# Two mixers in one program: the norm factors, the row factors and the first transposes at the passage from the first to the second

## The reference

```python
# end of the first block: mix is (512 x 2048)
out = jnp.einsum('bse,ed->bsd', mix, w_out[layer])
x = layer_norm(alpha * x + out, ln_g[layer], ln_b[layer])   # (u-mu)*rsqrt(var+eps)*g + b

# begin of the second block
mod = cond @ ada_w[i] + ada_b[i]
shift, scale, gate = jnp.split(mod, 3, axis=-1)
hdn = rms_norm_2(x, norm_g[i]) * (1.0 + scale[:, None, :]) + shift[:, None, :]
proj = h @ w_in                                             # h = hdn, w_in is 1024 x 6176
```

## Time and profile before

| what | us |
|---|---|
| median of 3 runs (lowest, highest) | 1112.73 (1109.14, 1112.83) |
| the profiled execution, device time | 1113.06 |
| its span in the profile | 1111.3 |
| TensorE matmul busy | 1067.0 (96%) |
| VectorE busy | 660.3 (59%) |
| ScalarE busy | 442.5 (40%) |
| GpSimd busy | 210.5 (19%) |

### The profile page before, as it was taken

How to read it: one execution, slowest core, us unless ns; L and a number is a source line. 1 busy time by engine, 2 the same in 40 slices (tenths; PEclk the granted TensorE clock), 3 DMA queues, 4 the chain that set the end, 5 groups by cost and what they waited for, 6 DMA issues and landing times. The chain is left out here.

```text
span 1111.3 us, 14437 instructions
## 1 busy us (share of the span) xinstructions
PE 1067.0 (96%) x5558; PEld 877.2 (79%) x5558; DVE 660.3 (59%) x1137; ACT 442.5 (40%) x824; POOL 210.5 (19%) x159
## 2 busy tenths in 40 slices
PE   7999999999989999989899999999999998999997
PEld 4888888888778867778778788887878876888886
DVE  4246435641156598655737865766594667876635
ACT  4223224332256553231523343348622447425432
POOL 0000000000000142201400100002104664135792
PEclk9999999999989999989999999999999999999999
DMA  8276534322132041132324345435211222203501
GB/s 298 82 265 226 202 114 133 114 76 94 30 123 58 19 177 39 38 128 81 118 81 151 114 150 190 153 114 171 84 68 45 89 95 76 76 20 98 188 1 77
DMA packets 58306, 123.89 MB, mean 111 GB/s; under 512 B 5760, under 2 KB 6016, under 8 KB 58112
## 3 DMA queue, kind: packets, MB, share of 16 engines
q1 hardware_dynamic: 55792, 110.22, 29.4%
q0 software_dynamic: 2304, 12.58, 3.2%
q10 hardware_dynamic: 144, 0.20, 0.0%
HBM read 108.83 MB, written 14.16 MB: 111 GB/s over the span
## 5 line engine op out<-in xcount | busy, mean ns | idle before, releaser
L287 DVE TENSOR_TENSOR w_lo<-raw,w_hi 128x2048 fp32r<-128x2048 f32 x58 | 135.6, 2337 | 214.7 <-ACT w_hi L283 203.6
L283 ACT ACTIVATE w_hi<-raw 128x2048 fp32r<-128x2048 f32 x51 | 97.6, 1913 | 220.8 <-PE projections_ps L131 138.3
L129 PE MATMUL projections_ps<-projections_x_hi,w_hi 128*128 128x512 f32 x208 | 81.1, 390 | 0.4 <-ACTq L503 0.4
L131 PE MATMUL projections_ps<-projections_x_hi,w_lo 128*128 128x512 f32 x208 | 80.9, 389 | 0.0
L130 PE MATMUL projections_ps<-projections_x_lo,w_hi 128*128 128x512 f32 x208 | 80.9, 389 | 0.0
L129 PE MATMUL projections_ps<-w_hi,projections_x_hi 128*128 128x512 f32 x192 | 74.7, 389 | 0.0
L130 PE MATMUL projections_ps<-w_lo,projections_x_hi 128*128 128x512 f32 x192 | 74.7, 389 | 0.0
L131 PE MATMUL projections_ps<-w_hi,projections_x_lo 128*128 128x512 f32 x192 | 74.7, 389 | 0.0
L244 DVE SCALAR_TENSOR_TENSOR resid<-resid,mixer_cw 128x512 f32<-128x512 f32 x96 | 65.0, 746 | 0.0
L2426 POOL TENSOR_TENSOR mixer_es<-masks,mixer_gsel 128x1024 f32<-128x1024 f32 x8 | 17.3, 2166 | 229.4 <-PE mixer_ps L1888 152.2
L129 PE MATMUL output_ps<-w_hi,output_m_hi 128*128 128x512 f32 x128 | 53.9, 421 | 0.7 <-DVE output_m_lo L1255 0.6
(11 more groups left out here) (324 smaller groups left out, 2568.6 us busy)
## 6 DMA issues: line engine op xcount, KB each, us to landing
raw<-in_w_in SPq DMA_DIRECT2D x26, 1024.0 KB, 5.0
raw<-in_gdn_w_in SPq DMA_DIRECT2D x24, 1024.0 KB, 5.0
tok<-in_ada_w POOLq DMA_DIRECT2D x16, 768.0 KB, 6.5
raw<-in_w_out SPq DMA_DIRECT2D x8, 1024.0 KB, 5.1
qkv_kept<-mixer_ring SPq DMA_DIRECT2D x8, 1024.0 KB, 4.2
mixer_st<-qkv_kept SPq DMA_DIRECT2D x32, 256.0 KB, 2.9
raw<-in_gdn_w_out SPq DMA_DIRECT2D x8, 1024.0 KB, 5.1
resid<-in_att_bias SPq DMA_DIRECT2D x16, 256.0 KB, 2.7
```

The costliest lines, as they stand in the source:

```text
L129: nc.tensor.matmul(out, w_hi, x_hi, start=first, stop=False, skip_group_check=True)
L131: return nc.tensor.matmul(out, w_lo, x_hi, start=False, stop=last, skip_group_check=True)
L283: self.nc.scalar.activation(self.hi[s][:], self.raw[s][:], ACT.Copy).then_inc(self.hi_ready, 1)
L287: engine.tensor_tensor(self.lo[s][:], self.raw[s][:], self.hi[s][:], ALU.subtract)\
```

## The change

- VectorE: `layer_norm(t)` does a tile in one go: add, statistics, aggregate, then it waits for the layer factor, then both products. Nothing of the next tile stands between them.
- GpSimd: the order is layer 0, last 0, layer 1, last 1, and so on; the counts in `LAYER_FACTOR` and `ROW_FACTOR` follow.
- ScalarE: the scaling of tile t follows the square of the same tile, for tiles 0 to 2, and is signalled (`next_ok`).
- TensorE: the transposes of tiles 0 to 2 of column blocks 0 to 3 (12 of 16) are issued at the end of the first block, behind the 48 small matmuls; in the second block `turn_x(e)` for e < 4 turns tile 3 alone. For that the PSUM tensor is one for both blocks, and the 48 matmuls go to bank 0 in place of bank 4.
- VectorE: the rest of the first weight unit of the second mixer is made as the last instruction of the first block, and not as the second of the second block.

```diff
-        LAYER_FACTOR, ROW_FACTOR = (3, 4, 6, 8), (5, 7, 9, 10)
+        next_ok = sem("next_ok")
+        LAYER_FACTOR, ROW_FACTOR = (3, 5, 7, 9), (4, 6, 8, 10)
...
             pe.wait_ge(mod_in, 16)
-            pe.wait_ge(added, GROUPS + 1)
+            pe.wait_ge(added, GROUPS + TT + 1)
             for j in range(3 * KT):
-                mm = nc.tensor.matmul(ps[:, 4, j:j + P], mod_acc[:, j * P:(j + 1) * P], ones, start=True, stop=True)
+                mm = nc.tensor.matmul(ps[:, 0, j:j + P], mod_acc[:, j * P:(j + 1) * P], ones, start=True, stop=True)
             mm.then_inc(mod_sum, 1)
+            for t in range(TT - 1):
+                pe.wait_ge(next_ok, t + 1)
+                for e in range(4):
+                    tr = nc.tensor.transpose(ps[:, 4 + e, t * P:(t + 1) * P], tok[:, t, e * P:(e + 1) * P], ident)
...
-                if t:
-                    act.wait_ge(factor_ok, ROW_FACTOR[t - 1])
-                    nc.scalar.activation(tok[:, t - 1, 0:D_MODEL], resid[:, t - 1, :], ACT.Copy, scale=row_f[:, t - 1:t])
+                if t < TT - 1:
+                    act.wait_ge(factor_ok, ROW_FACTOR[t])
+                    nc.scalar.activation(tok[:, t, 0:D_MODEL], resid[:, t, :], ACT.Copy, scale=row_f[:, t:t + 1])\
+                        .then_inc(next_ok, 1)
...
-            layer_factor(0)
             for t in range(TT):
-                if t + 1 < TT:
-                    layer_factor(t + 1)
+                layer_factor(t)
                 last_factor(t)
...
-            def before_factor(t):
+            def layer_norm(t):
...
-                dve.wait_ge(var_ok, t + 1)
+                dve.wait_ge(factor_ok, LAYER_FACTOR[t])
                 own.did(nc.vector.scalar_tensor_tensor(out=resid[:, t, :], in0=resid[:, t, :],
                                                        scalar=mean_var[:, t, 0:1], in1=row_g[:],
                                                        op0=ALU.subtract, op1=ALU.mult))
-                return own.n
-            def after_factor(t, step):
-                dve.wait_ge(factor_ok, LAYER_FACTOR[t])
-                own.wait(step)
+                own.wait()
                 nc.vector.scalar_tensor_tensor(out=resid[:, t, :], in0=resid[:, t, :], scalar=ln_f[:, t:t + 1],
                                                in1=row_b[:], op0=ALU.mult, op1=ALU.add).then_inc(normed, 1)
-            step = before_factor(0)
             for t in range(TT):
-                next_step = before_factor(t + 1) if t + 1 < TT else None
-                after_factor(t, step)
-                step = next_step
+                layer_norm(t)
...
+            dve.wait_ge(w.hi_ready, len(OUT_UNITS) + 1)
+            nc.vector.tensor_tensor(w.lo[0][:], raw[0][:], w.hi[0][:], ALU.subtract).then_inc(w.lo_ready, 1)
... second_mixer
-                for t in range(TT):
+                for t in range(TT - 1 if e < 4 else 0, TT):
...
-            dve.sem_inc(w.lo_ready, 2)
+            dve.sem_inc(w.lo_ready, 3)
             nc.vector.tensor_scalar(xn[:, TT - 1, :], resid[:, TT - 1, :], row_f[:, TT - 1:TT], None, ALU.mult).then_inc(xn_ok, 1)
-            w.rest(nc.vector, dve, 0, 0)
```

More of the change, by code:

```diff
@@ L172, in build @@
                 attention(nc, a, ahead, mix_in, raw, m_g, resid, masks, qk, vals, tok, bias_in)
-            scan_and_output(nc, a, ahead, wba, wba_in, mix_in, split, raw, att_f, m_g, masks, small, resid, row_f, tok, xbc, dt,
+            ps = ctx.enter_context(nc.psum_tensor("ps", [P, 8, COLS], F32))
+            scan_and_output(nc, a, ps, ahead, wba, wba_in, mix_in, split, raw, att_f, m_g, masks, small, resid, row_f, tok, xbc, dt,
                             adt, modc, g_col, gain)
-        second_mixer(nc, a, ahead, wba, wba_in, split, raw, masks, resid, row_f, modc, gain, small, tok)
+        second_mixer(nc, a, ps, ahead, wba, wba_in, split, raw, masks, resid, row_f, modc, gain, small, tok)
 def spare_buffers(resid):
@@ L858, in _, with scan_and_output @@
                     exponentials(a_next, TILES[3:])
-def scan_and_output(nc, a, ahead, wba, wba_in, mix_in, split, raw, att_f, m_g, masks, small, resid, row_f, tok, xbc, dt, adt, modc,
+def scan_and_output(nc, a, ps, ahead, wba, wba_in, mix_in, split, raw, att_f, m_g, masks, small, resid, row_f, tok, xbc, dt, adt, modc,
                     g_col, gain):
@@ L906, in scan_and_output @@
         mod_acc = xbc[:].rearrange("p a b -> p (a b)")[:, 0:3 * D_MODEL]
-        ps = ctx.psum("ps", [P, 8, COLS], F32)
         ps_x = ps[:, X, :].rearrange("p (h c) -> p h c", c=HD)
@@ L1178, in _ @@
                     act.wait_ge(w.units_used, 9)
-                    nc.scalar.activation(w.hi[0][:], raw[0][:], ACT.Copy)
+                    nc.scalar.activation(w.hi[0][:], raw[0][:], ACT.Copy).then_inc(w.hi_ready, 1)
                 act.wait_ge(normed, t + 1)
@@ L1393, in before_factor @@
                                                        op0=ALU.subtract, op1=ALU.mult))
-                return own.n
-            def after_factor(t, step):
-                dve.wait_ge(factor_ok, LAYER_FACTOR[t])
-                own.wait(step)
+                own.wait()
                 nc.vector.scalar_tensor_tensor(out=resid[:, t, :], in0=resid[:, t, :], scalar=ln_f[:, t:t + 1],
                                                in1=row_b[:], op0=ALU.mult, op1=ALU.add).then_inc(normed, 1)
-            step = before_factor(0)
             for t in range(TT):
-                next_step = before_factor(t + 1) if t + 1 < TT else None
-                after_factor(t, step)
-                step = next_step
+                layer_norm(t)
             dve.wait_ge(mod_sum, 1)
-            own.did(nc.vector.tensor_tensor(modc[:], ps[:, 4, 0:3 * KT], mod_b[:], ALU.add))
+            own.did(nc.vector.tensor_tensor(modc[:], ps[:, 0, 0:3 * KT], mod_b[:], ALU.add))
             own.wait()
@@ L1411, in _, with second_mixer @@
                                            op0=ALU.add, op1=ALU.mult)
-def second_mixer(nc, a, ahead, wba, wba_in, split, raw, masks, resid, row_f, modc, gain, small, z):
+            dve.wait_ge(w.hi_ready, len(OUT_UNITS) + 1)
+            nc.vector.tensor_tensor(w.lo[0][:], raw[0][:], w.hi[0][:], ALU.subtract).then_inc(w.lo_ready, 1)
+def second_mixer(nc, a, ps, ahead, wba, wba_in, split, raw, masks, resid, row_f, modc, gain, small, z):
     w_in = a["gdn_w_in"][0].rearrange("(k p) c -> p k c", p=P)
@@ L1515, in second_mixer @@
         scratch = [flat(ktok[:].rearrange("p j c e -> p (j c) e"))[:, D_MODEL * n:D_MODEL * (n + 1)] for n in range(2)]
-        ps = ctx.psum("ps", [P, 8, COLS])
         Z_BANKS = (0, 1) * 4 + (6, 7, 2, 3, 4, 5, 0, 1)
```

## The result

The changed kernel takes 1116.09 us (median of 6 runs, 1110.9 to 1117.44) where the kernel before took 1112.28 beside it (6 runs, 1109.14 to 1112.83). The ratio is 1.0046, 95% interval 1.0024 to 1.0067: slower by 0.2 to 0.7%. The profiled execution took 1115.69, its span is 1113.9 against 1111.3.

What follows compares the result with a forecast made beforehand. TensorE, busy 96% of the span, was taken as the bound, so a later first product of the second mixer counts one to one. Block +3.25, transposes -0.97 and clock +0.8 gave +3.1 on 1112.73: 1115.8 us, range 1112.0 to 1119.0.

Steps and rivals of the forecast that it cites:

- The serial chain: VectorE's tiles in the first block: waiting for each layer factor makes a tile 5.21, last product +2.43 us.
- The rest: End of the first block: VectorE's moved rest holds up GpSimd's last row factor, another +1.2 us, bounds 0.5 to 1.2.
- forecast of the block: End of the first block, up to VectorE's last scaling: closes 3.25 us later than before.
- Rival C: End of the first block: the rest does not hold GpSimd; block +2.5, total +2.4, 1115.1 us; chance 0.15.
- The transposes: Start of the second mixer: 12 of 16 transposes done earlier shorten scaling to first product, -0.97 us.
- The clock: TensorE's restart in the second mixer: products may first run at half clock, +0.8 us, bounds 0 to about 1.2.
- rival A: Second mixer: thinner restart keeps TensorE's clock low longer; +5.6 to +7.1 us, about 1119; chance 0.15.
- The sum: Whole run: +3.25 - 0.97 + 0.8 = +3.1 us, 1115.8 on the median's basis.
- Rival B: VectorE's tiles in the first block: VectorE does not fall behind; -0.9, about 1111.8 us; chance 0.10.
- Bank 0: The 48 small matmuls in the first block: the added wait is met 13 us ahead and costs nothing.

Runs made afterwards that it cites:

- order_back: Changed kernel with VectorE's old interleaved order and GpSimd's old order of factors; ratio to the kernel before 1.0048 (1.0023 to 1.0073).
- turns_back: Changed kernel with all 16 first transposes in the second block again; ratio to the kernel before 1.0046 (1.0018 to 1.0074).
- rest_back: Changed kernel with the rest of the first weight unit made in the second block again; ratio to the kernel before 1.0076 (1.0049 to 1.0104).
- no_clash: Changed kernel with GpSimd's old order alone, layer factor t+1 ahead of row factor t; ratio to the kernel before 1.0032 (1.0012 to 1.0053).
- busy_both: Changed kernel with unused small matmuls in both TensorE holes, 19 behind the moved transposes, 8 behind tile 3's; ratio to the kernel before 1.0027 (1.0008 to 1.0046).
- before_busy: Kernel before with 12 unused small matmuls behind the modulation sum, timed twice; ratios to the kernel before 0.9987 and 0.9990, both intervals containing 1.
- busy_pe_18: Changed kernel with 18 unused small matmuls behind the moved transposes; ratio to the kernel before 1.0045 (1.0022 to 1.0068).
- busy_pe: Changed kernel with 40 unused small matmuls behind the moved transposes; ratio to the kernel before 1.0079 (1.0048 to 1.0109).
- rest_only: Kernel before with only the rest of the first weight unit moved to VectorE's last instruction of the first block; ratio 1.0019 (1.0000 to 1.0037).

## Why the prediction was right, and which term was mis-sized

Forecast 1115.8, slower by 3.1; measured 1116.09, slower by 3.8 beside its own kernel before (1112.28 over six runs, where the forecast started from 1112.73 over three; part of the closeness of the two times is that). The direction and its main mechanism are shown by runs.

- **The serial chain.** Worked out: 5.21 a tile, tile 3's add at 16.35, last product 22.00 (+2.43). Measured: 5.20, 16.50, 22.23 (+2.66). order_back takes all of it away; turns_back and rest_back, which leave the order of the tiles alone, keep it (22.25). The queueing behind row factors was put at 0.36 in tile 1, and was 0.45 there: GpSimd begins 0.09 after its previous power, which I had left out.
- **The rest.** Worked out +1.2 on the last row factor through the hold on GpSimd; rest_back measured 1.05. This cost hangs on the timing: in order_back and no_clash the same rest is over before the factor starts, and costs it nothing. The forecast of the block (+3.25) met +3.32 for VectorE's last scaling. Rival C (no hold) is refuted.
- **The transposes.** -0.97 forecast on P1; from VectorE's last scaling to P1 the changed kernel takes 3.01 against 3.88, -0.87. turns_back gives 1.07.
- **The clock was the mis-sized term.** I took +0.8, bounded by 1.2, on the ground that the half clock would last as long as before. From P1 to P2 it measured +1.92, and 1.9 over the whole passage by busy_both and before_busy, so the bound failed as well. What failed is "the length of the old stretch": that length had followed a dense restart, and the change made the restart thin. That was rival A's mechanism, at less than half of its price (1.1 on top of the 0.8, where A had at least 2.5), and A's own sign did not appear: the clock was back 4.1 us after the first product, not more than 5. With +1.92 in the sum in place of 0.8, the passage would have come out at +4.2 for the measured +4.37.
- **The sum** came out near the measured difference with luck. In the profiles the short clock term and the one half-clock stretch less behind the passage have opposite signs: +4.37 in the passage, +2.6 in the span. The medians' +3.8 lies between, and its interval (2.7 to 7.5 us) holds the passage's figure too. How much of the total is the passage and how much the luck of later stretches the times cannot tell.
- **Rival B** (no falling behind) is refuted by the adds at 5.20, 10.86 and 16.50. Its price had also left the clock term out, though the restart would be as thin in it.
- **Bank 0** cost nothing, as forecast: the 48 small matmuls start 13.40 after tile 0's add, as before (536.37 and 536.82 on the two profiles).

Where the gain that the change was after went: the factor did become cheap (0.83 for 2.83 of GpSimd's time), tile 3's own chain from add to last product went from 5.97 to 5.73. But this 0.24 was bought with 2.9 us of lateness at its start. The 1.07 of the early transposes was paid back by the clock, and the moved rest landed on GpSimd's last row factor, which ends the block.

## What to carry to other kernels

Before making an engine wait for a short factor "because the factor is then cheap", add up the engine's cycle per tile with the wait in it and compare it with the rate at which its tiles arrive: here 4.16 became 5.20 against 4.53, and a hidden cost became an exposed one in every tile. When work is moved out of the restart after an idle stretch, look at what is left: a dense half-clock stretch that lies in cheap work can be shorter and cheaper than a thin one that reaches into the products. And an instruction moved "into a gap" has to be checked against every engine that it can block, not only its own queue.

## What the runs showed of the hardware that was not expected

- Two short idle times can be followed by the lower clock if the work between them is thin. With TensorE idle for 2.07, four transposes, and idle for 1.42, it went to 0.50 (busy_pe_18); with 1.21, four transposes and 1.42 it stayed at 1.00 (busy_pe), and also with 1.75, sixteen transposes and 0.98 (before_busy). The Trainium skill, "TensorE: Matmul & The Clock Gate", Part 1, section "HAM oscillation — how this bites in real kernels", describes a kernel in which each group of matmuls is followed by a wait of some 3 to 5 us for a DMA, and whose clock falls every time. The trace agrees that the clock falls after pauses, and shows it after shorter ones, the 2.07 and 1.42 above.
- The clock returned 3.8 us after the restart when TensorE was busy throughout (turns_back, after 7.77 idle), and 7.1 us after it when it was busy for 5.96 of these (the changed kernel, after 6.08 idle). Transposes alone bring it back: in turns_back it rose at 554.76, and the first product started at 554.93.
- GpSimd's multiply-add of 128 x 1 (0.19 alone) ends just behind the VectorE instruction that holds it up: 545.94 against 545.88 in rest_only, 547.74 against 547.69 in the changed kernel. Other instructions end later after the hold: the power (0.55 alone) 0.41 after VectorE's product, the larger product 0.90 after the rest.
- A small float32 matmul of the modulation sum leaves two records in the profile (24 matmuls, 48 records, 5.52 us), a transpose of the same shape one. Sizing filler by the count of records makes it twice too long.
